# Row sums of the second PSUM bank in the other two column groups, and half of tile 0's last down product moved ahead of tile 1's layers

## What is computed

```
def block_fn(hb):                      # a block of 128 tokens
    ...
    u = expert_u[experts]
    vsel = expert_v[experts]
    act = jax.nn.gelu(jnp.einsum('thkd,td->thk', u, hb), approximate=False)
    return jnp.einsum('thk,thkd->td', gate * act, vsel)
...
x = x + mod[:, 5] * peer_ffn(h2, ...)          # end of the first block
# second block, layer 0: short convolution, memory attention, swiglu
# second block, layer 1: block attention, memory attention, swiglu
def swiglu(h, w_gu, w_down):
    g, u = jnp.split(h @ w_gu, 2, axis=-1)
    return (jax.nn.silu(g) * u) @ w_down
return rms_norm_2(x, norm_final)
```

## Time and profile before

| | us |
|---|---|
| median of 3 runs (lowest, highest) | 1775.55 (1775.13, 1777.11) |
| the profiled execution | 1777.88 |
| its span, from the first instruction to the last | 1776.1 |
| PE busy in the span | 1605.0 |
| DVE, ACT, POOL busy | 750.1, 501.5, 289.9 |
| granted TensorE clock, mean | 0.96 |
| moved by DMA | 595.22 MB |

### The profile page before, as it was taken

How to read it: one execution, slowest core, us unless ns; L and a number is a source line. 1 busy time by engine, 2 the same in 40 slices (tenths; PEclk the granted TensorE clock), 3 DMA queues, 4 the chain that set the end, 5 groups by cost and what they waited for, 6 DMA issues and landing times.

```text
span 1776.1 us, 15554 instructions
## 1 busy us (share of the span) xinstructions
PE 1605.0 (90%) x5460; PEld 750.2 (42%) x5460; DVE 750.1 (42%) x1807; ACT 501.5 (28%) x1283; POOL 289.9 (16%) x268
## 2 busy tenths in 40 slices
PE   6998989588659998699899997989999999999998
PEld 3444456155225453234343333443344544455443
DVE  3653035776686545754534446542212100031101
ACT  3311123322333323424344133433411210122210
POOL 1000001223443323222211222221100000000000
PEclk8999989789889999899899998999999999999999
DMA  9555165999999999999999999999967677765774
GB/s 353 184 189 189 72 236 234 422 370 420 421 415 385 408 421 421 414 421 420 396 422 421 420 421 419 406 413 421 407 261 271 237 287 294 296 235 225 284 289 185
DMA packets 94957, 595.22 MB, mean 335 GB/s; under 512 B 7024, under 2 KB 7024, under 8 KB 28192
## 3 DMA queue, kind: packets, MB, share of 16 engines
q1 hardware_dynamic: 56576, 319.28, 45.9%
q0 software_dynamic: 37584, 270.75, 37.2%
q10 hardware_dynamic: 720, 4.19, 0.6%
HBM read 593.15 MB, written 1.05 MB: 335 GB/s over the span
## 4 chain that ended last, share of the span: by engine, by line
PE 78%; DMA 11%; DVE 6%; issue 2%; ACT 2%; POOL 1%; SPq 0%; DVEq 0%; POOLq 0%; ACTq 0%
PE bank L971 35%; PE bank L1132 9%; PE bank L1049 8%; DMA arena<-in_peer_rows,pidx 8%; PE bank L681 7%; PE bank L947 3%; PE bank L758 2%; PE bank L936 2%; DMA ring<-in_weights 2%; PE bank L978 2%; DVE arena L2076 2%; DMA ring<-in_w_mod 1%; PE bank L735 1%; PE bank L653 1%; PE bank L1031 1%
## 5 line engine op out<-in xcount | busy, mean ns | idle before, releaser
L1606 POOL DMA_INDIRECT arena<-in_peer_rows,pidx x256 | 285.1, 1113 | 951.6 <-PE bank L1132 622.5
L2076 DVE SCALAR_TENSOR_TENSOR arena<-arena,ring 128x1024 f32<-128x1024 f32 x256 | 307.5, 1223 | 142.7 <-DMA arena<-in_peer_rows,pidx 140.5
L1132 PE MATMUL bank<-arena,keep 128*32 128x512 f32 x1024 | 263.5, 655 | 84.9 <-ACT keep L1564 84.9
L971 PE MATMUL bank<-ring,arena 128*128 128x512 f32 x736 | 319.4, 593 | 0.0
L971 PE MATMUL bank<-ring,hT_all 128*128 128x512 f32 x544 | 239.3, 595 | 2.9 <-issue 2.5
L971 PEld LDWEIGHTS bank<-ring,arena 128*128 128x128 f32 x736 | 138.5, 190 | 168.8 <-issue 168.7
L971 PEld LDWEIGHTS bank<-ring,hT_all 128*128 128x128 f32 x544 | 101.3, 190 | 134.2 <-issue 132.1
L1132 PEld LDWEIGHTS bank<-arena,keep 128*32 128x32 f32 x1024 | 50.8, 115 | 244.9 <-issue 131.4
L1551 ACT ACTIVATE pf<-pf 128x2 f32<-128x2 f32 x128 | 25.9, 203 | 409.0 <-DVE arena L2076 408.8
L2191 DVE TENSOR_TENSOR x_all<-x_all,bank 128x512 f32<-128x512 f32 x40 | 27.5, 688 | 201.8 <-PE bank L1049 107.6
L681 PE MATMUL bank<-ring,hT_all 128*128 128x512 f32 x192 | 88.8, 621 | 3.0 <-DVE hT_all L1683 3.0
(11 more groups left out here) (369 smaller groups left out, 1560.8 us busy)
## 6 DMA issues: line engine op xcount, KB each, us to landing
ring<-in_weights SPq DMA_DIRECT2D x126, 2048.0 KB
ring<-in_w_mod SPq DMA_DIRECT2D x12, 2048.0 KB
ring<-in_w_in SPq DMA_DIRECT2D x6, 2048.0 KB
ring<-in_weights SPq DMA_DIRECT2D x8, 1024.0 KB
arena<-in_peer_rows,pidx POOLq DMA_INDIRECT x256
ring<-in_weights SPq DMA_DIRECT2D x8, 512.0 KB
mem_all<-in_b_mod POOLq DMA_DIRECT2D x3, 512.0 KB, 9.8
hT_all<-in_xT ACTq DMA_DIRECT2D x1, 1024.0 KB, 7.5
```

The costliest lines, as they stand in the source:

```text
L971: m = mm(b[:, :], src[:, k], slot8[w][:, k], start=(k == 0), stop=(k == KC - 1))
L1132: m = mm(acc[b][r:r + 32, :], diag[n % 8], vslot[n % SLOTS][:, b * 512:(b + 1) * 512], start=(n % 128 < 4), stop=(n % 128 >= 124))
L1606: nc.gpsimd.indirect_dma_start(out=row_in[n % SLOTS], out_offset=None, in_=a["peer_rows"], in_offset=bass.IndirectOffsetOnAxis(ap=pidx[:, ...
L2076: stt(uslot[n % SLOTS], uslot[n % SLOTS], 1.0, h2g[n % 4], ALU.mult, ALU.mult, accum_out=pact2[:, 16 * (g % 2) + k:16 * (g % 2) + k + 1]). ...
```

## The change

Three edits. The partition at which a matmul of bank 1 begins is shifted by 64: picks n and n+1 add to column groups r and r+32 in bank 0 and to the other two of the four groups in bank 1. `add_experts` puts the halves of bank 1 back in place with two operations of 64 partitions where one of 128 stood. `PICK_US` goes from 5.2 to 5.8, and of tile 0's last down product the parts 0 to 2 go under the rows, while 3 to 5 remain as fills. With `PICK_US` the steps under the rows stand at the same picks as before at first, and up to 4 picks earlier at the end, which leaves room for the three parts at picks 250 and 252.

```
-LAYER_FIRST, PICK_US = 136, 5.2
-UNDER_ROWS, DOWN = [], [f"dn1 {c}" for c in range(6)]
+LAYER_FIRST, PICK_US = 136, 5.8
+UNDER_ROWS, DOWN = [], [f"dn1 {c}" for c in range(3, 6)]
...
-FILLS = {"turn conv": ["dn1 0"], "cin 2": ["dn1 1"], "pturn0 0": ["dn1 2"], "bk 0": ["dn1 3"], "bpturn 0": ["dn1 4"], "pturn1 0": ["dn1 5"],
-         "gu1 3": ["final 0"]}
+FILLS = {"cin 2": ["dn1 3"], "pturn0 0": ["dn1 4"], "pturn1 0": ["dn1 5"], "gu1 3": ["final 0"]}
...
                 for b in range(2):
                     for n in (n0, n0 + 1):
-                        r = 32 * (n % 4)
+                        r = 32 * ((n + 2 * b) % 4)
                         m = mm(acc[b][r:r + 32, :], diag[n % 8], vslot[n % SLOTS][:, b * 512:(b + 1) * 512],
...
-                    link(tt(part, acc[half][:, :], g5row[:, c], ALU.mult))
+                    if half == 0:
+                        link(tt(part, acc[0][:, :], g5row[:, c], ALU.mult))
+                    else:
+                        tt(part[0:64], acc[1][64:128, :], g5row[0:64, c], ALU.mult)
+                        link(tt(part[64:128], acc[1][0:64, :], g5row[64:128, c], ALU.mult))
                     tt(x[:, t, c], x[:, t, c], part, ALU.add).then_inc(experts_added[t], 1)
```

## The result

The change made the kernel slightly slower: 1779.67 us (median of 20 runs) against 1776.31 us for before in the same runs, a ratio of 1.0022 with a 95% interval of 1.0012 to 1.0032. The forecast was 1768.3, with a range of 1760 to 1778. One of the 20 executions of before took 2431 us; it hardly moves the median and is left out of the ratio.

A forecast was written before the change was run, and what follows sets the result against it. Under the rows the DMA, full at 421 GB/s, was taken as the limit with PE close; afterwards PE. +0.5 under the rows and -7.8 after gave -7.3, so 1768.3 us from the median 1775.55; range 1760 to 1778.

The forecast's parts named there:

- The sum under the rows: Under the rows: 10.5 us paid for the moved parts' bytes less 10 us of idle DMA regained, +0.5 us.
- 10 us back: Under the rows, shorter pairs regain 10 us of the 21.2 us of idle DMA, with bounds 0 and 21.
- The column groups: At L1132, four matmuls run together: a pair falls from 1.84 to 0.94 us, saving 115 us of PE work.
- The moves of the other steps by up to 4 picks change neither bytes nor sum: Under the rows, placing the other steps up to 4 picks differently costs nothing.
- by pair 246 only two of the three blocks are extra in the ring: Near the last rows, 3.67 MB of the parts' 5.77 MB are extra by then, 8.7 us.
- The three parts' bytes, +10.5: Under the rows, the moved parts' 5.77 MB cost between 8.7 and 13.7 us of full DMA; 10.5 taken.
- the DMA gives nothing back: Rival: DVE and ACT chains and starts set the idle DMA; 3 us come back, time 1777; chance 0.13.
- After the rows: Behind the last pair, three fills fewer remove 18.9 us of PE work but uncover waits; net -7.8 us.
- pturn0 0: After the rows: the fill here becomes a full part, 6.9 instead of 5.15 us; +1.7 us.
- bk 0: After the rows: the fill ahead goes, -6.9, with 0.6 us of wait exposed; net -6.3 us.
- bpturn 0: After the rows: without the fill PE waits for the softmax, then 1.5 us for slow matmuls; net +0.6 us.
- turn conv: After the rows: the fill ahead goes, -6.9, with 3.1 us of waiting for `x` exposed; net -3.8 us.

The follow-up runs named there:

- experiment 3: The whole change, except that all six down parts stay fills and none is moved; 1784.91 us, ratio 1.0054 to before.
- the groups alone: Before with only the column groups and the split of `add_experts`, step order and all six fills as before; 1774.01 us against 1775.85, ratio 0.999.
- experiment 8: The groups alone, with only the steps from layer 1's memory attention on at picks of 5.8 us; 1783.32 us, ratio 1.0046 to before.
- experiment 9: The groups alone, with only the steps ahead of layer 1's memory attention at picks of 5.8 us; 1774.28 us, ratio 0.9987 to before.
- experiment 5: The whole change, but steps at picks of 5.2 us as before and the three moved parts ahead of the last pair; 1779.93 us, ratio 1.003 to before.
- experiment 4: Column groups, steps at 5.2 us a pick, one down part moved under the rows, no fill ahead of `bk 0`; 1768.26 us, ratio 0.9956 to before.
- experiment 10: Groups, picks of 5.2 us, two down parts ahead of the last pair, no fill at `turn conv` and `bk 0`; 1773.62 us, ratio 0.999 to before.
- experiment 7: The groups alone, with seven of eight DVE operations of the memory's scaling left out; 1768.82 us, ratio 0.9962 to before.
- experiment 11: Experiment 4 with the pair in two column groups as before; 1776.13 us, ratio 1.0006 to before.
- experiment 6: The groups alone, with each matmul of a pair issued twice; 1780.05 us, ratio 1.003 to before.

## Why the prediction was wrong

**The sum under the rows: +0.5 forecast, +11.7 in the profiled execution.** Idle DMA was to shrink by 10 us and grew by 3.5. The bytes ahead of the last landing were to cost 10.5 and cost 7.4. From the landing to the last pair 0.8 came on top. So in the sum the term that made the miss is "10 us back"; the other step that failed, the order of the steps, says where the bytes came from.

**The column groups: right.** 1.00 us a pair, where 0.92 to 0.99 was derived and 0.94 taken; the shorter pair with two banks, which no row had shown, overlaps. Four groups give 3.4 times here (8 records of 0.43 us one after the other would be 3.43 us), between the 3.7 of L653 and the 3.07 that the Trainium skill (TensorE: Matmul & The Clock Gate, part 3) has for four row groups.

**"The moves of the other steps by up to 4 picks change neither bytes nor sum": this step failed.** They change no bytes of the program, but they change which bytes stand ahead of the last row. Experiment 3 measures the order at about +11 us against the groups alone, with no part moved, and experiments 8 and 9 put it all on the last steps: with those, 2.6 MB more of the ring (6.2 us at 421.5 GB/s) are in by the last landing, and the last row lands 8 us later after the first issue (995.2 against 987.1). I had written the right fact down for the parts ("by pair 246 only two of the three blocks are extra in the ring") and not asked who had brought them there. In the sum the error was hidden, because the price set for the parts' bytes stood in its place. Nor did the order alone decide the sign: experiment 5 has the old order, and is slower than before too.

**The three parts' bytes, +10.5: the size was not far off, the cause another.** The change has 3.1 MB more ahead of the last landing, 7.4 us, and 2.6 MB of them come by the order alone (experiment 3). But experiments 4, 5 and 10 move one to three parts and have 137.6 to 137.8 MB: a part ahead of the last pairs brings no bytes in front of the rows. What three parts cost there is PE time, 12 us more behind the landing than one part. So with the new order or with all three parts at the last pair the loss is about the same (3.9 and 5.3 us), the one mostly in DMA, the other in PE.

**"10 us back" of the idle DMA: this step failed, and it made the miss.** Measured against before: none. Idle is 21.6 us with the groups alone and 24.7 in the change, against 21.2. I took a busy PE in a stretch with idle DMA for its cause, at 525 to 555 us above all. Experiment 7 shows DVE's scaling as the cause there with the groups in place (that it was so in before as well is argued from it); for the other stretches the cause stays open. In the change a lower clock (0.84 in that stretch, 0.97 before) goes with it, and what that costs no run separates. Of the rivals, "the DMA gives nothing back" came true in its main term; it had 0.13, and its 1777 left out the order.

**What the groups are worth.** The prediction had no place for it: behind the last landing PE is the limit, with up to three pairs and whatever stands between them (in before it is busy 7.7 of 7.9 us there). The groups gave 3.7 us there alone, which left PE busy only 2.4 of 4.3 us. With a down part among the pairs they were worth 9 (experiments 4 and 11), 6.6 of it behind the landing, mostly because PE reaches the landing with less left to do.

**After the rows: -7.8 forecast, -5.8 measured in the change, -7.8 in experiment 5**, which has the same fills (479.4 us against 487.2), and mostly by the terms. PE at the places, in the change, answering to the earlier trace rows:

```profile
1392.08 7.03 PE L1048 MATMUL bank<-ring,s_all 128*128 128x512 f32 x16
...
1400.95 1.24 PE L1030 MATMUL bank<-arena,mem_all 128*128 128x128 f32 x9 [0.97 <-ACT arena L1179]
...
1537.60 0.66 PE L977 MATMUL bank<-keep,x_all 128*128 128x128 f32 x4 [0.41 <-DVE x_all L2194]
1538.84 6.68 PE L970 MATMUL bank<-ring,arena 128*128 128x512 f32 x15 [0.59 <-issue]
...
1591.36 3.68 PE L977 MATMUL bank<-keep,arena 128*128 128x128 f32 x16 [4.63 <-DVE arena L2255]
1594.83 0.64 PE L1086 MATMUL bank<-arena,s_all 128*128 128x128 f32 x2
```

- `pturn0 0`: +2.1 (from the start of the scores to the first product behind, 13.97 to 16.05), forecast +1.7.
- `bk 0`: -6.1 (8.37 to 2.26 from the first transpose to the first product), forecast -6.3; the wait is the 0.59 that was read off.
- `bpturn 0`: 0.0 (16.09 us from the first score to the product behind, before and after), forecast +0.6. PE idles 4.63 us and then works slowly, as said.
- `turn conv`: -1.8, forecast -3.8. The transposes end 4.3 us behind the last pair, as derived (4.0). The rest is the clock: the fill behind the two waits of 1.5 us takes 8.73 us. Experiment 5 has the same two waits, its fill takes 7.03, and the place gives -3.6 there. So the reading of the waits was right, and the slow fill belongs to this execution of the change; what brought the clock down there stays open.

## What to carry to other kernels

Where a transfer queue is full, cost a reordering by what it puts ahead of the transfer that ends last, not by what it adds in all: here steps moved forward by a few picks brought their weights in front of the last rows although the total was unchanged. Look for the short stretch behind the last landing; there the compute engine is the limit again, and an edit worth nothing on average (the shorter pair) is what makes room for work there, about one down part of it here. A busy engine in a stretch with idle DMA is not yet the cause: shorten it and look, before counting the idle time as gain.

## What the runs showed of the hardware

Eight matmuls of 32 columns in four column groups, two PSUM banks in turn (experiment 6), take 1.88 us from start to start, where the eight of L653 in one bank took 1.85, so a second bank costs the overlap next to nothing:

```profile
1265.26 1.94 PE L1133 MATMUL bank<-arena,keep 128*32 128x512 f32 x16
1267.14 0.66 PE L978 MATMUL bank<-keep,s_all 128*128 128x128 f32 x4
```

The granted clock was 0.50 at the start of the fill behind the two waits of 1.58 and 1.49 us in the change (the columns as in the earlier trace rows):

```profile
1306.00:1309.00 3.00, 3.00 (x5) 1.01 (x4) 0.15 (x1) 2.97 (x8) 0.00 (x0) 0.50 0.63 257
```

Experiment 5 has the same waits with the same 0.66 us of transposes between them, and its clock stays at 1.00:

```profile
1297.92 0.66 PE L979 MATMUL bank<-keep,x_all 128*128 128x128 f32 x4 [1.57 <-DVE x_all L2092]
1300.07 0.66 PE L979 MATMUL bank<-keep,x_all 128*128 128x128 f32 x4 [1.49 <-DVE x_all L2092]
1300.56 7.03 PE L1050 MATMUL bank<-ring,s_all 128*128 128x512 f32 x16
```

Experiment 10 shows the same (1.57 and 1.49 us, clock 1.00). So two such waits do not by themselves bring the clock down, and a slow stretch seen once is not yet a price of the waits in front of it.
